# Experts' up weights in eight consecutive rows a partition, in a two-block transformer kernel

## What is computed

```python
h2 = rmsnorm(x, norm2_g) * (1.0 + sc2) + sh2
...
xs = h[tok]                                  # rows of h2, sorted by expert
a = lax.ragged_dot(xs, w1, sizes)
b = lax.ragged_dot(xs, w3, sizes)
y = lax.ragged_dot(jax.nn.silu(a) * b, w2, sizes)
y = (y * weights[order][:, None]).astype(h.dtype)
return jax.ops.segment_sum(y, tok, num_segments=N)
```

## Time and profile before

| | |
|---|---|
| Median of 3 runs | 3686.57 us (3684.36 to 3690.19) |
| The profiled execution: its own time | 3680.95 us |
| Its span, first to last instruction | 3679.1 us |
| TensorE busy | 3479.0 us, 95% of the span |
| VectorE, ScalarE busy | 1700.5 us, 887.9 us |
| Mean granted clock of TensorE | 0.967 of full speed |
| DMA over the whole span | 511.79 MB, mean 139 GB/s |

### The profile page before, as it was taken

How to read it: one execution, slowest core, us unless ns; L and a number is a source line. 1 busy time by engine, 2 the same in 40 slices (tenths; PEclk the granted TensorE clock), 3 DMA queues, 4 the chain that set the end, 5 groups by cost and what they waited for, 6 DMA issues and landing times. The chain is left out here.

```text
span 3679.1 us, 44601 instructions
## 1 busy us (share of the span) xinstructions
PE 3479.0 (95%) x17639; PEld 1818.2 (49%) x17639; DVE 1700.5 (46%) x2976; ACT 887.9 (24%) x1842; POOL 440.7 (12%) x329
## 2 busy tenths in 40 slices
PE   7999999999999798998989999998889999999999
PEld 4544444555555443433354578566554444444444
DVE  3589999655566400000023355545543434443246
ACT  2311110544332211111133122222433211111001
POOL 0033451222000011111101111111000000000000
PEclk9999999999999799999989999998899999999999
DMA  5223221221555699999953232212122011111434
GB/s 183 81 77 126 100 106 38 83 70 24 180 182 212 213 363 383 382 384 382 348 196 107 73 110 69 88 53 82 38 84 89 23 46 46 46 38 43 140 114 163
DMA packets 274728, 511.79 MB, mean 139 GB/s; under 512 B 21228, under 2 KB 100164, under 8 KB 269166
## 3 DMA queue, kind: packets, MB, share of 16 engines
q1 hardware_dynamic: 259550, 467.71, 36.0%
q0 software_dynamic: 10416, 35.15, 3.3%
q10 hardware_dynamic: 4576, 6.33, 0.5%
HBM read 449.84 MB, written 59.30 MB: 138 GB/s over the span
## 5 line engine op out<-in xcount | busy, mean ns | idle before, releaser
L600 PE MATMUL ch_side<-aT,space 128*128 128x512 f32 x896 | 394.0, 598 | 0.0
L1862 PE MATMUL jn_duo<-space,dsa 128*128 128x512 f32 (+1 forms) x736 | 335.6, 610 | 5.7 <-ACT dsa L1939 3.1
L600 PEld LDWEIGHTS ch_side<-aT,space 128*128 128x128 f32 x896 | 169.0, 191 | 213.9 <-issue 211.9
L1969 DVE SCALAR_TENSOR_TENSOR dsa<-jn_duo,ex_weight,ex_gate 128x1024 f32<-128x1024 f32 x24 | 30.8, 1284 | 527.2 <-PE jn_duo L1881 527.2
L3175 PE MATMUL en_bank<-en_h,en_up 128*128 128x512 f32 x528 | 233.8, 592 | 0.0
L1862 PEld LDWEIGHTS jn_duo<-space,dsa 128*128 128x128 f32 (+1 forms) x736 | 125.8, 175 | 152.7 <-issue 152.7
L726 DVE MAX8 ch_best<-ch_score 128x8 f32<-128x384 f32 (+5 forms) x192 | 171.6, 894 | 6.1
L2344 PE MATMUL mx_duo<-mx_chunks,mx_region 128*128 128x512 f32 x384 | 170.8, 598 | 0.4 <-ACT space L2614 0.4
L1862 PE MATMUL jn_duo<-aT,dsa 128*64 128x512 f32 (+1 forms) x288 | 140.8, 647 | 30.2 <-DMA space<-exp_w 28.4
L727 DVE MATCH_REPLACE8 ch_score<-ch_best,ch_score 128x384 f32<-128x384 f32 (+5 forms) x192 | 168.1, 875 | 0.0
L3175 PEld LDWEIGHTS en_bank<-en_h,en_up 128*128 128x128 f32 x528 | 100.2, 190 | 125.8 <-issue 125.8
(11 more groups left out here) (562 smaller groups left out, 5714.8 us busy)
## 6 DMA issues: line engine op xcount, KB each, us to landing
space<-exp_w SPq DMA_DIRECT2D x62, 2048.0 KB, 22.1
aT<-exp_w SPq DMA_DIRECT2D x34, 2048.0 KB, 19.9
en_up<-w_down SPq DMA_DIRECT2D x132, 256.0 KB, 3.5
space<-ada_w SPq DMA_DIRECT2D x12, 2048.0 KB, 8.8
space<-w_ada SPq DMA_DIRECT2D x12, 2048.0 KB, 8.3
space<-proj_padded SPq DMA_DIRECT2D x96, 256.0 KB, 3.6
aT<-w_in SPq DMA_DIRECT2D x7, 2048.0 KB, 8.6
en_up<-w_gate SPq DMA_DIRECT2D x22, 512.0 KB, 4.8
```

What stands on the lines that cost most here:

```text
L600: last = nc.tensor.matmul(side_ps[i % 2][:, :], hT[:, k, t * P:(t + 1) * P], w[n % 2][:, k, :], start=k == 0, stop=k == KD - 1)
L1862: last = nc.tensor.matmul(ps[mine, :], xT[:, k, mine], up_view(ring[place])[:, k, :], start=k == 0, stop=k == KD - 1)
```

## The change

The up loads take the layout that the down loads have: `"(p k) f"`, partition `p` holds rows `8p` to `8p+7` of the expert's matrix. So `xT[:, k, :]` has to hold the columns `8p + k` of the rows, and `flip_x` reads every eighth column of `x[b]`. The affine vectors have to follow, as element `8p + k` in partition `p`, column `k`. They are reordered once: at the start of joining TensorE transposes both into `bank[7]`, ScalarE copies them to `affine_rows` and stores them to a scratch tensor in HBM, and loads them back in the new order two tiles later into `affine`, which the experts' stage reads. The router's part of joining keeps the old vectors.

```diff
@@ joining
+        affine_rows, affine = sb("affine_rows", [KD, 2, P]), sb("affine", [P, 2, KD])
+        affine_turned, affine_copied, affine_stored, affine_loaded = (sem(f"affine_{n}") for n in ("turned", "copied", "stored", "loaded"))
-        then = experts(nc, g, ctx, space, dsa, aT, duo, gain)
+        then = experts(nc, g, ctx, space, dsa, aT, duo, affine, affine_loaded)
@@ joining, sync
-            sp.dma_start(up_view(ring[0]), g.d["exp_w1"][0, 0].rearrange("(k p) f -> p k f", p=P)).then_inc(g.ring_loaded[0], 16)
-            sp.dma_start(up_view(ring[1]), g.d["exp_w3"][0, 0].rearrange("(k p) f -> p k f", p=P)).then_inc(g.ring_loaded[1], 16)
+            sp.dma_start(up_view(ring[0]), g.d["exp_w1"][0, 0].rearrange("(p k) f -> p k f", p=P)).then_inc(g.ring_loaded[0], 16)
+            sp.dma_start(up_view(ring[1]), g.d["exp_w3"][0, 0].rearrange("(p k) f -> p k f", p=P)).then_inc(g.ring_loaded[1], 16)
@@ joining, tensor
             last.then_inc(gate_row, 1)
+            pe.wait_ge(gained, 1)
+            nc.tensor.transpose(bank[7][0:KD, 0:P], gain[:, :], g.ident[:, :])
+            nc.tensor.transpose(bank[7][0:KD, P:2 * P], shift, g.ident[:, :]).then_inc(affine_turned, 1)
             merge(0, 0)
             merge(0, 1)
             merge(1, 0)
+            pe.wait_ge(affine_copied, 1)
             flip_m(0)
@@ joining, scalar
+            act.wait_ge(affine_turned, 1)
+            nc.scalar.copy(affine_rows[:, :, :].rearrange("k n p -> k (n p)"), bank[7][0:KD, 0:2 * P]).then_inc(affine_copied, 1)
             open_gate(0)
+            act.wait_ge(affine_copied, 1)
+            act.dma_start(g.d["affine"].rearrange("n (k p) -> k n p", p=P), affine_rows[:, :, :]).then_inc(affine_stored, 16)
             for t in range(NT + 2):
+                if t == 2:
+                    act.wait_ge(affine_stored, 16)
+                    act.dma_start(affine[:, :, :], g.d["affine"].rearrange("n (p k) -> p n k", p=P)).then_inc(affine_loaded, 16)
@@ experts
-    shift = g.modT[:, 24:24 + KD]
+    gain, shift = affine[:, 0, :], affine[:, 1, :]
-            order = "e (k p) f -> p e k f" if view is up_view else "e (p k) f -> p e k f"
-            src = wd[0].rearrange(order, p=P)[:, bass.ds(expert, 1), :, :]
+            src = wd[0].rearrange("e (p k) f -> p e k f", p=P)[:, bass.ds(expert, 1), :, :]
@@ experts, flip_x
-                last = nc.tensor.transpose(x_ps[:, k, :], x[b][:, k * P:(k + 1) * P], g.ident[:, :])
+                last = nc.tensor.transpose(x_ps[:, k, :], x[b].rearrange("p (n k) -> p k n", n=P)[:, k, :], g.ident[:, :])
@@ experts, scalar and vector, ahead of the first affine step
+        act.wait_ge(affine_loaded, 16)
+        dve.wait_ge(affine_loaded, 16)
```

More of the change, by code:

```diff
@@ L1705, with experts @@
     pass
-def experts(nc, g, ctx, space, dsa, aT, duo, gain):
+def experts(nc, g, ctx, space, dsa, aT, duo, affine, affine_loaded):
     then = Engines()
@@ L3614, in program @@
         d["moe_w"] = scratch("moe_w", (SLOTS, 1))
+        d["affine"] = scratch("affine", (2, D))
         d["proj2_padded"] = scratch("proj2_padded", (CONV - 1 + S, N2))
```

## The result

The changed kernel takes 3656.13 us (median of 4 runs, 3651.87 to 3659.26), the kernel before 3688.07 us beside it (median of 4, 3684.36 to 3690.19; the 3686.57 given ahead is the median of the first three of these). The ratio is 0.9913, 95% interval 0.9900 to 0.9926: 32 us faster, 27 to 37 with the interval. Predicted were 3658.5 us and 28.1 us.

What follows compares the result with a forecast made beforehand. The experts' stage was taken as DMA-bound, TensorE close behind. Loads -30.2, hand-over +1.3, first flip +0.5, affine transposes +0.3 make -28.1 us: 3680.95 becomes 3652.9, and 5.6 for the median gives 3658.5 us; range 3643 to 3675.

Steps and rivals of the forecast that it cites:

- The bound: Experts' stage: transfers bind and cost 44.0 us in all; TensorE's own pace is 6 to 7 us a turn behind.
- The size of the gain: Experts' up loads: 16 KB pieces save 0.54 us a load, over 56 loads ahead of the last wait, 30.2 us.
- Remaining waits: Experts' stage: of TensorE's 44.0 us lost to transfers 13.8 stay, some 2 us a turn; listed waits fall to some 10.
- The hand-over, +1.3 us: Experts' stage: loads waiting for TensorE to release buffers, as around 1291 us, may come once more and lose 1.3 us.
- The flips: Experts' transposes of x at 32 byte steps: 9 ns more each, 0.2 us a turn, hidden; 0.5 us at the first.
- B: Experts' flips bind in part, above 74 ns extra each; at 157 ns the gain is 15.5 us, 3671.1; chance 0.14.
- C: Experts' flips cost over 0.30 us a transpose, so the stage is slower; at 0.35 us 16.9 us slower, 3703.5; chance 0.04.
- The affine step: Start of joining: two more TensorE transposes cost 0.3 us; ScalarE's copies are covered by 2.9 us and cost 0.
- POOL's transfers: Experts' stage: gathers wait more often behind 16 KB pieces, but 17.4 us from issue to use covers them; cost 0.
- A: Experts' stage: 16 KB pieces run so much faster that all TensorE's waits go and it binds; 3643.4 us; chance 0.11.
- D: Experts' up loads: half the fixed cost is not per packet, so half the saving goes; 13.0 us gained, 3673.6; chance 0.09.
- E: Experts' up loads: the source side holds all at 387 GB/s, so no gain; 0.8 us of cost left, 3687.4; chance 0.06.

Runs made afterwards that it cites:

- e8: The changed kernel with down loads of half their size, old data in the rest of each buffer: ratio 0.9871, 47.6 us faster than the kernel before.
- e10: The changed kernel, unchanged, run and profiled a second time: ratio 0.9934, 24.3 us faster than the kernel before.
- e2: The kernel before with only the up loads in 16 KB runs, plain flips and old affine vectors: ratio 0.9921, 29.1 us faster.
- e1: The kernel before with only the flips of every eighth column, loads and affine vectors as they were: ratio 1.0009, 3.3 us slower.
- e7: The changed kernel with each partition's eight rows written to its buffer in reverse order, so 2 KB pieces again: ratio 1.0010, 3.7 us slower than before.
- e5: The changed kernel with up weights in runs of two rows, 4 KB, and flips to match: ratio 0.9942, 21.4 us faster than the kernel before.
- e6: The changed kernel with up weights in runs of four rows, 8 KB, and flips to match: ratio 0.9932, 25.1 us faster than the kernel before.

## Why the prediction was right, step by step

- **The bound.** Right. Forecast: DMA-bound, TensorE's floor 7 x 66.84 = 467.9 us for the loop. `e8` ran it in 468.5; the 0.6 us more fit the flips, 0.09 us a turn.
- **The size of the gain.** Right: 0.54 us a load from the earlier trace rows, 56 loads, 30.2 us. The place to measure it is the product with w3 in the eighth turn, ahead of which the 56 loads were counted: it came 521.7 us behind the first paired up product before (five profiles, 519.6 to 522.9) and 492.4 in the change (three, 492.2 to 492.7), 29.3 us earlier. In the loop alone the gain was 509.1 to 482.4, 26.7 us. The stage gained 29.7, but its end depends on where the last wait falls (25.5 us behind w3, or 28.2 to 29.2), so that agreement to half a microsecond is partly luck.
- **Remaining waits.** Forecast 13.8 us of lost time, "some 10" in the list of waits; the list has 11.2. The loop stood 12.6 us above its floor in the first profile and 16.1 in `e10`. Turns of 69.5 us were forecast, 68.7 came (481.1 / 7); the last paired up product was forecast near 1771 and starts at 1773.14.
- **The hand-over, +1.3 us.** Not seen as a loss. The 0.9 us between 30.2 and 29.3 leave room for most of it; nothing tests it alone.
- **The flips.** The 9 ns a transpose taken from `flip_act` was too much: 4 ns on the mean (117.0 for 112.6), 0.1 us a turn for the 0.2 forecast. That it hides in the waits is borne out beside 16 KB pieces (`e2`) and not settled beside 2 KB pieces (`e1`, `e7`). Rivals B and C are out, as they needed 74 and 300 ns. The Trainium skill's cacheline rule ("SBUF — State Buffer", Door 1) has four fp32 elements free and charges more than four. The weight loads here do not follow it: two and four elements give 207 and 206 ns, eight 192 ns, plain 144.
- **The affine step.** 0.3 us was forecast on TensorE, 0.22 us shown, nothing in the time. ScalarE's cover of 2.9 us was 4.2 (963.6 to 967.85) in the execution with the lower clock, 3.4 (962.7 to 966.07) in `e10`.
- **POOL's transfers.** As forecast: later (median 11.3 us for 6.8), the worst no worse (12.3 for 12.5). The median came back in the second profiles, 7.0 before and 11.4 after. From issue to use there are 17.4 us or more in 23 of the 24 blocks. The prediction overlooked the last block, where it was 5.8 us before and is 7.5 now; even so all 24 of VectorE's products waited for TensorE and none for its gather.
- **Rivals.** A (TensorE binds) is out: 11.2 us of waits for loads stay, and `e8` shows what they are worth. D is out: 4 KB and 8 KB packets took what a fixed 9.4 ns says. By an estimate from the Trainium skill's 3 cycles a packet ("DMA: Bandwidth & Descriptors", Why small descriptors are slow) the 56 loads would have gained about 12 us; the measurement decides against it, with 29.3 us up to w3. E is out: 434 GB/s with 16 KB pieces.
- **The sum.** -28.1 us for -32 measured, inside the interval of 27 to 37. The 4 us between are within what runs differ by: the same change gave -29.1 in `e2` and -24.3 in `e10`.

## What to carry to other kernels

When a stage runs with the DMA share at one and an engine waits for loads, look for a load in the same stage whose runs are longer and take the price per piece from two stretches of the same trace; here that gave the gain up to the last of these loads to 1 us (30.2 for 29.3). Choose the row order so that one partition's piece is consecutive both in HBM and in SBUF, since either alone was worth nothing here (HBM alone in `e7`, SBUF alone in the kernel before), and move the permutation to an access pattern that is read anyway. Compare profiles by stage and in more than one execution: here the difference of one profile each was 10 us off, partly because one wait of 3 to 6 us came or did not come at the stage's end.

## What the runs showed of the hardware

- A packet took 84.7, 160.0, 310.1 and about 612 ns of a DMA engine at 2, 4, 8 and 16 KB (`e5`, `e6`), which makes 387, 410, 423 and 430 GB/s for the core. That is 75 ns for each 2 KB and a fixed 9 to 10 ns a packet.
- TensorE's weight load of 128 columns, read with a step of 2, 4 or 8 fp32 elements, took 207, 206 and 192 ns (`flip_x` of `e5`, `flip_act`, `flip_x` of after; 209 ns in `flip_x` of `e6`, a step of 4), plain 140 to 144 ns. Most of that was hidden in a row of transposes, but not all. A turn at TensorE's pace has 24 transposes of `flip_x` and took 66.84 us plain, 66.93 with a step of 8 and 67.13 with a step of 2: 4 and 12 ns a transpose.

```profile
L1884 PEld LDWEIGHTS jn_duo<-ident,dsa 128*128 128x128 f32 x200 | 27.6, 207 | 15.7 <-issue 14.0 <-DMA dsa<-xn,entries 1.6
```

The row is `e5`'s, with a step of 2, and so is its first turn in the table by windows:

```profile
1289.68:1356.81 67.13, 67.13 (x230) 29.30 (x229) 5.64 (x6) 13.33 (x31) 11.89 (x15) 1.00 1.00 375
```

- TensorE's granted clock fell after waits for loads and came back: 0.98 and 0.97 in turns with waits, 1.00 in turns without. At the stage's end the same work kept TensorE busy for 26.18 us at a mean clock of 0.88 and for 22.95 at 1.00 (after and `e5`).
